# Index scores in units of two heads, their products with the low key parts each on half of TensorE's rows

## The reference, cut to what matters

```python
adm = (kpos[None, :] // CHUNK) <= (qpos[:, None] // CHUNK)
isc = jnp.einsum('bqhd,bsd->bqhs', qib, k_idx) * (IDX_DIM ** -0.5)
score = jnp.einsum('bqhs,bqh->bqs', jax.nn.relu(isc), wb * (IDX_HEADS ** -0.5))
score = jnp.where(adm[None], score, NEG)
_, idx = lax.top_k(score, n_sel)
```

## Time and profile before

| | us |
|---|---|
| median of three runs | 3438.98 (3437.29 to 3440.9) |
| the profiled execution, its own time | 3442.62 |
| its span in the trace | 3440.8 |
| TensorE busy (PE) | 3356.9, 98% |
| VectorE busy (DVE) | 1940.1, 56% |
| ScalarE busy (ACT) | 1450.8, 42% |
| GpSimd busy (POOL) | 1610.3, 47% |

### The profile page before, as it was taken

One profiled execution on the slowest core, in us unless ns is written; L12 is line 12 of the kernel. 1 busy time (PEld: TensorE's weight loads), 2 busy tenths in 40 slices (PEclk: granted clock), 3 DMA queues, 4 the chain that ended last, 5 costly groups with the idle time before them and its releaser, 6 DMA issues.

```text
span 3440.8 us, 44189 instructions
## 1 busy us (share of the span) xinstructions
PE 3356.9 (98%) x16616; PEld 2774.7 (81%) x16616; DVE 1940.1 (56%) x3380; ACT 1450.8 (42%) x2601; POOL 1610.3 (47%) x949
## 2 busy tenths in 40 slices
PE   7999999999999999999999999999999999999998
PEld 6778878878887888888788878977887789878787
DVE  3236647558565566457667755766768478621112
ACT  3224435345444443245455434735654357420001
POOL 4555554454325555522555552044556510356665
PEclk9999999999999999999999999999999999999999
DMA  4745454444433333323433232063233400432332
GB/s 135 208 138 167 113 168 129 130 129 142 165 105 127 100 103 96 115 75 135 140 94 109 93 110 87 1 216 97 92 103 100 148 32 1 136 103 92 93 103 92
DMA packets 446564, 389.04 MB, mean 113 GB/s; under 512 B 20977, under 2 KB 376561, under 8 KB 445713
## 3 DMA queue, kind: packets, MB, share of 16 engines
q1 hardware_dynamic: 424736, 348.04, 33.1%
q10 hardware_dynamic: 21616, 38.17, 3.1%
HBM read 323.37 MB, written 62.78 MB: 112 GB/s over the span
## 4 chain that ended last, share of the span: by engine, by line
PE 90%; DVE 3%; ACT 3%; issue 1%; DMA 1%; POOL 1%; ACTq 0%; SPq 0%; DVEq 0%; POOLq 0%
PE BANK L800 20%; PE BANK L801 20%; PE BANK L802 20%; PE LP L800 3%; PE LP L802 3%; PE LP L801 3%; PE BANK L1013 3%; PE BANK L1028 2%; PE LP L990 2%; PE LP L991 2%; PE BANK L1030 2%; PE LP L892 2%; PE LP L891 2%; PE LP L996 1%; PE BANK L1039 1%
## 5 line engine op out<-in xcount | busy, mean ns | idle before, releaser
L768 POOL TENSOR_SCALAR WHI<-WRAW 128x1024 fp32r<-128x1024 f32 x456 | 494.8, 1085 | 1424.4 <-PE BANK L802 1164.7
L770 POOL TENSOR_TENSOR WLO<-WRAW,WHI 128x1024 fp32r<-128x1024 f32 x456 | 1108.7, 2431 | 38.0
L800 PE MATMUL BANK<-H2hi,WHI 128*128 128x512 f32 x1408 | 565.5, 402 | 3.6 <-DVE X L2036 3.6
L801 PE MATMUL BANK<-H2lo,WHI 128*128 128x512 f32 x1408 | 558.2, 396 | 0.0
L802 PE MATMUL BANK<-H2hi,WLO 128*128 128x512 f32 x1408 | 557.4, 396 | 0.0
L800 PE MATMUL BANK<-HThi,WHI 128*128 128x512 f32 (+1 forms) x1024 | 408.9, 399 | 1.8 <-DVE QS L1634 1.8
L801 PE MATMUL BANK<-HTlo,WHI 128*128 128x512 f32 (+1 forms) x1024 | 404.9, 395 | 0.0
L802 PE MATMUL BANK<-HThi,WLO 128*128 128x512 f32 (+1 forms) x1024 | 404.6, 395 | 0.0
L1384 ACT ACTIVATE MASK<-SCD,THR 128x896 bf16<-128x896 f32 (+5 forms) x186 | 281.9, 1516 | 227.3 <-DVE THR L1693 199.7
L802 PEld LDWEIGHTS BANK<-H2hi,WLO 128*128 128x128 f32 x1408 | 265.3, 188 | 65.0
L800 PEld LDWEIGHTS BANK<-H2hi,WHI 128*128 128x128 f32 x1408 | 265.8, 189 | 62.7 <-DVE X L2036 4.5
(11 more groups left out here) (279 smaller groups left out, 6504.7 us busy)
## 6 DMA issues: line engine op xcount, KB each, us to landing
WRAW<-in_w_in SPq DMA_DIRECT2D x124, 512.0 KB, 4.4
WRAW<-in_w_ffn_gate SPq DMA_DIRECT2D x88, 512.0 KB, 3.8
WRAW<-in_w_ffn_up SPq DMA_DIRECT2D x88, 512.0 KB, 3.8
WRAW<-in_w_ffn_down SPq DMA_DIRECT2D x88, 512.0 KB, 3.8
qsp<-QS SPq DMA_DIRECT2D x32, 512.0 KB, 5.7
gates<-GS ACTq DMA_DIRECT2D x64, 256.0 KB, 2.1
WRAW<-in_w_out SPq DMA_DIRECT2D x32, 512.0 KB, 4.1
GL<-gates ACTq DMA_DIRECT2D x48, 256.0 KB, 4.1
```

The lines of the kernel that those rows point to most:

```text
L768: nc.gpsimd.tensor_scalar(hi, raw, 1.0, 1.0, ALU.mult, ALU.mult).then_inc(w_hi, 1)
L770: nc.gpsimd.tensor_tensor(lo, raw, hi.bitcast(f32), ALU.subtract).then_inc(w_split, 1)
L800: nc.tensor.matmul(dst, whi, mhi, start=first, stop=False)
L801: nc.tensor.matmul(dst, whi, mlo, start=False, stop=False)
```

## The change

A unit is now two heads (2m and 2m + 1) of one query tile over up to 512 keys, each head in a bank of its own of the LP buffer. The two products with KIhi stay as they were, over 128 rows. Of the products with KIlo only the query's high part is kept, 64 rows: for the even head rows 0 to 63, for the odd head rows 64 to 127. The product of low query by low key is left out. In the built program these two matmuls carry the position (0, 0) and (64, 0) and the size 64 by 128. The relu takes both heads in one instruction, the additions are two per unit, each of up to 512 columns.

```diff
         def score_units(b):
-            return [(b, j, h, c, w) for j in searched(b) for h in range(HEADS) for c, w in chunks(width_of(b, j))]
+            return [(b, j, m, c, min(ROWS, width_of(b, j) - c)) for j in searched(b) for m in range(HEADS // 2)
+                    for c in range(0, width_of(b, j), ROWS)]
...
-                for _, j, h, c, w in score_units(b):
-                    dst = take("logits", relu_ready, (b, j, h, c), ("idx", b, j, h, c))
-                    for a, v in halves(c, w):
-                        q = Q[:, h, j * P:(j + 1) * P]
-                        nc.tensor.matmul(dst[:, a - c:a - c + v], q, KIhi[:, a:a + v], start=True, stop=False)
-                        last = nc.tensor.matmul(dst[:, a - c:a - c + v], q, KIlo[:, a:a + v], start=False, stop=True)
-                    last.then_inc(logits_full, made(logits_full, ("idx", b, j, h, c)))
+                for _, j, m, c, w in score_units(b):
+                    dst = take("logits", relu_ready, (b, j, m, c), ("idx", b, j, m, c))
+                    for s in range(2):
+                        nc.tensor.matmul(dst[:, s * ROWS:s * ROWS + w], Q[:, 2 * m + s, j * P:(j + 1) * P], KIhi[:, c:c + w],
+                                         start=True, stop=False)
+                    for s in range(2):
+                        r = slice(s * HD, (s + 1) * HD)
+                        nc.tensor.matmul(dst[:, s * ROWS:s * ROWS + w], Q[r, 2 * m + s, j * P:(j + 1) * P], KIlo[r, c:c + w],
+                                         start=False, stop=True).then_inc(logits_full, 1)
+                    made(logits_full, ("idx", b, j, m, c), 2)
                     yield
...
                     if g >= 2:
-                        act.wait_ge(score_added, g - 1)
+                        act.wait_ge(score_added, 2 * (g - 1))
                     act.wait_ge(logits_full, n(logits_full, ("idx",) + key))
-                    nc.scalar.activation(RB[:, g % 2, 0:w], logits(("idx",) + key)[:, 0:w], ACT.Relu
+                    pair = logits(("idx",) + key)[:, :].rearrange("p (s c) -> p s c", s=2)
+                    nc.scalar.activation(RB[:, g % 2, :].rearrange("p (s c) -> p s c", s=2)[:, :, 0:w], pair[:, :, 0:w], ACT.Relu
                                          ).then_inc(relu_ready, made(relu_ready, key))
...
-                    r, iw = RB[:, g % 2, 0:w], IW[:, j, h:h + 1]
                     s = scores_at(b, j)[:, c:c + w]
...
+                    for h in (2 * m, 2 * m + 1):
+                        r, iw = RB[:, g % 2, h % 2 * ROWS:h % 2 * ROWS + w], IW[:, j, h:h + 1]
+                        if h == 0:
+                            ins = nc.vector.tensor_scalar(s, r, iw, None, ALU.mult)
+                        else:
+                            dve.wait_ge(score_added, n(score_added, (b, j, h - 1, c)))
+                            ins = nc.vector.scalar_tensor_tensor(s, r, iw, s, ALU.mult, ALU.add)
+                        ins.then_inc(score_added, made(score_added, (b, j, h, c)))
```

More of the change, by code:

```diff
@@ L1365, in relus @@
             def relus(b):
-                for _, j, h, c, w in score_units(b):
-                    key = (b, j, h, c)
+                for _, j, m, c, w in score_units(b):
+                    key = (b, j, m, c)
                     g = n(relu_ready, key) - 1
                     if g >= 2:
-                        act.wait_ge(score_added, g - 1)
+                        act.wait_ge(score_added, 2 * (g - 1))
                     act.wait_ge(logits_full, n(logits_full, ("idx",) + key))
-                    nc.scalar.activation(RB[:, g % 2, 0:w], logits(("idx",) + key)[:, 0:w], ACT.Relu
+                    pair = logits(("idx",) + key)[:, :].rearrange("p (s c) -> p s c", s=2)
+                    nc.scalar.activation(RB[:, g % 2, :].rearrange("p (s c) -> p s c", s=2)[:, :, 0:w], pair[:, :, 0:w], ACT.Relu
                                          ).then_inc(relu_ready, made(relu_ready, key))
@@ L1868, in sums @@
             def sums(b):
-                for _, j, h, c, w in score_units(b):
-                    if (h, c) == (0, 0) and j == searched(b)[0]:
+                for _, j, m, c, w in score_units(b):
+                    if (m, c) == (0, 0) and j == searched(b)[0]:
                         dve.wait_ge(iw_ready, n(iw_ready, b))
@@ L1875, in sums @@
                             dve.wait_ge(sc_out, n(sc_out, (b - 1, JT - 1)))
-                    key = (b, j, h, c)
-                    g = n(relu_ready, key) - 1
+                    g = n(relu_ready, (b, j, m, c)) - 1
                     dve.wait_ge(relu_ready, g + 1)
-                    r, iw = RB[:, g % 2, 0:w], IW[:, j, h:h + 1]
                     s = scores_at(b, j)[:, c:c + w]
[L1881 to L1886, removed]
+                    for h in (2 * m, 2 * m + 1):
[6 more added lines that the diff above has]
+                        ins.then_inc(score_added, made(score_added, (b, j, h, c)))
                     top = width_of(b, j)
                     if h == HEADS - 1 and c + w == top:
-                        dve.wait_ge(score_added, n(score_added, key))
+                        dve.wait_ge(score_added, n(score_added, (b, j, h, c)))
                         nc.vector.memset(scores_at(b, j)[0:HD, top - HD:top], NEG).then_inc(score_ready, made(score_ready, (b, j)))
```

## The result

| | before | after |
|---|---|---|
| median, us | 3438.14 (4 runs, 3437.05 to 3440.9) | 3464.73 (4 runs, 3460.47 to 3465.52) |
| the profiled execution, its own time | 3442.62 | 3460.47 |
| its span in the trace | 3440.8 | 3458.6 |
| granted clock, mean over the span | 0.994 | 0.996 |

The ratio is 1.0073, 95% interval 1.0061 to 1.0085: 26.6 us slower, with 21 to 29 us as the interval. I had forecast 3481 with a range of 3452 to 3500. The sign and the range were right, the size was too large by 16 us. The third rival, "the low pair starts together", had 3464.

The account below looks back on a forecast made before the run. TensorE was taken as the bound; four unit sizes added 29.1, 5.0, 4.4 and 3.5 us, 42 in sum, so 3439 + 42 = 3481 us (chance 0.50), with a range of 3452 to 3500.

Parts of the forecast that it names:

- The third rival: Score matmuls: both low matmuls of a unit start together, the second low load costing nothing; +25, 3464 us, chance 0.10.
- TensorE sets the pace: Block 3's score slots: PE busy 159.65 of 160 us, so a unit's PE time changes the span while DVE keeps up.
- What bounds the gain: 31 us: Score matmuls: two 64-row matmuls side by side save one step of four per unit, at most 31 us in all.
- The drain of 0.09 and the open load of 0.11: At each change between 128 and 64 rows: 0.09 us running out, then 0.11 us loading; read at the L940 transposes.
- rival 1: Changes of size in a unit: no drain there, so the kernel gets faster, 3418 to 3428 us; chance 0.16.
- rival 5: Score units: neither drain nor overlap, four steps as before; 3439 us, chance 0.07.
- I stay with 0.11: Low pair: the second low matmul starts 0.11 us after the first, for its load; 152 x 0.11 = 17 us.
- m + 2s + 0.51: Predicted unit time in us: m the step between the high matmuls, s the time one matmul's columns are taken in.
- Rival 2: Low pair: the two low matmuls run one after the other without overlap; +55, 3494 us, chance 0.12.
- VectorE costs nothing: Block 3: five units take DVE 9.94 us against PE's 11.5, so the longer PE stretch covers DVE's extra 14 us.
- rival 4: Block 3: DVE becomes the bound, its doubled additions each meeting a stall, 12.5 us per five units; +52, 3491, chance 0.05.
- 2.4 us of stall: Block 3's last query tile before: four additions in a row take 1.89 us each, not 1.28; the excess was left in.

Follow-up runs that it names:

- experiment 1: The changed kernel with the low products of both heads again over 128 rows, units still in pairs of heads: 3441.67 us, ratio 1.0011.
- Experiment 2: The kernel before, units of one head, with both high matmuls first, then the low ones on that head's 64 rows: 3503.38 us, ratio 1.0190.
- experiment 3: The changed kernel with two units issued together, four high matmuls then two low pairs, per change to 64 rows: 3461.46 us, ratio 1.0071.

## Why the prediction was right in its sign and too large

**TensorE sets the pace.** Right. PE is busy 159.95 of 160 us in block 3, the time followed PE's work to 2 us (27.9 worked out, 26.6 measured), and experiment 1 brought it back with that work.

**What bounds the gain: 31 us.** Right: the pair overlaps fully, a unit of 512 keys has three steps and two changes, 3 x 0.23 + 2 x 0.20 = 1.09.

**The drain of 0.09 and the open load of 0.11, taken from one place with 8 rows and plain float32.** Right, though it was one case of another type and size. Into the low pair it is 650.70 - 650.61 = 0.09; out of it, the L895 truly start at 650.70 + 0.11 and have their columns in at 651.03, and the load starts at 651.13: 0.10. The open load behind it is 651.24 - 651.13 = 0.11. That a price of 8 rows holds for 64 the prediction could only assume; here it does. Experiment 2 gives the same 0.40 for both changes with no overlap in it. The rule of the Trainium skill (TensorEngine Tiling (Array Packing), section Tiling Modes), that a change of tiling mode drains TensorE, is borne out here for 64 rows; the price is that of these rows. With that rival 1, no drain, falls, and rival 5 with it.

**"I stay with 0.11 because that is the distance of two loads right behind such a change".** This is the step that failed. The 0.11 between two loads in the earlier trace rows belongs to two loads on the same rows: experiment 2 has it again (0.29 us for the two, 0.19 for one). After the change they stand on different rows, and the two loads and the two matmuls start together, 4 ns apart. So a unit is m + 2s + 0.40 instead of m + 2s + 0.51: 1.07, 0.905, 0.74 and 0.62 us, where the trace has 1.086, 0.918, 0.749 and 0.627. The term was 152 x 0.11 = 17 us and measured about nothing; 42 - 17 = 25. The 4 ns of the Trainium skill (TensorE: Matmul & The Clock Gate, section Packing small matmuls) are what the trace shows, and the estimate of +26 by that page was the better one. I had the two values side by side and gave 0.50 to the one from this kernel's rows and 0.10 to the other; but the row didn't show the case in question, loads on separate rows.

**Rival 2, one after the other.** Fell; what it would have looked like is experiment 2.

**VectorE costs nothing, rival 4.** Right in what it costs, not in all of its parts. These are additions of the last query tile after, for the earlier trace rows, in the timeline, merged and then one by one with what GpSimd does beside them, and in the groups by shape:

```profile
866.06 10.08 DVE L1890 SCALAR_TENSOR_TENSOR SCP<-RB,IW,SCP 128x512 f32<-128x512 f32 x10 [1.20 <-ACT RB L1377]
877.08 10.08 DVE L1890 SCALAR_TENSOR_TENSOR SCP<-RB,IW,SCP 128x512 f32<-128x512 f32 x10 [0.94 <-ACT RB L1377]
```

```profile
867.05 2.69 POOL L771 TENSOR_TENSOR WLO<-WRAW,WHI 128x1024 fp32r<-128x1024 f32 x1
867.54 2.75 DVE L1890 SCALAR_TENSOR_TENSOR SCP<-RB,IW,SCP 128x512 f32<-128x512 f32 x1
870.22 0.74 DVE L1890 SCALAR_TENSOR_TENSOR SCP<-RB,IW,SCP 128x512 f32<-128x512 f32 x1
```

```profile
L1890 DVE SCALAR_TENSOR_TENSOR SCP<-RB,IW,SCP 128x512 f32<-128x512 f32 x189 | 204.7, 1091 | 56.5 <-ACT RB L1377 52.3
```

Five units take VectorE 10.08 us (predicted 9.94) and TensorE 877.08 - 866.06 = 11.02 us (predicted 11.5), so there is 0.9 us of slack. The mean of an addition is 1.09 us, but few take that long: eight of the ten in the first row take 0.75, as one does alone, and two take 1.45 and 2.75, while GpSimd splits a weight piece. It is so in the whole trace after: of the 196 additions of 512 columns (7 of them in block 0) 144 take 0.75 us and none of them overlaps an L771; the 52 longer ones all do. This is also the "2.4 us of stall" that the prediction left as it was: of its "1.89 each" before, the four take 1.82, 3.43, 1.27 and 1.27 us. It was right to leave it, and rival 4's reason, a stall for each of twice as many instructions, doesn't hold: there is one split a job, however many additions stand beside it. That the one engine holds up the other is argued from this overlap; no run took the splits away.

From block 3's sum of squares to the end of its last addition VectorE is busy for 124.20 us before and 139.96 after, 16 more where I had 14. Over the whole kernel it is 38.5 more, since blocks 0 to 2 have 64 additional instructions as well, which I didn't count. PE didn't wait for it beyond the 0.5 us above. The cover that I named, TensorE's longer slot, is what hides this: with the slot back at 10.2 us, experiment 1 shows 2.4 us of waits, and in experiment 3 VectorE becomes part of the bound.

**The signs named for the trace.** The load of the first L895 starts 0.31 us after the second L891 (some 0.3 predicted); the next matmul of the job truly starts at 651.24, 0.42 after the L895's 650.70 + 0.11 (0.4); PE is busy for 99% in block 2 (233.98 of the 235 us from 483 on); no waits for RB beyond that half microsecond. Two missed: the distance of the two L895, and the second phase "as long as before", which was 7 us shorter in the profiled execution by the granted clock alone.

## What to carry to other kernels

Splitting TensorE's rows for a pair of small matmuls saves one matmul per pair and costs a way in and a way out: 0.23 against 0.40 us here with 512 columns of fp32r, so two pairs per stay only break even. Fewer columns didn't help: a unit lost 0.17 us with 512 columns, 0.24 with 384, 0.28 with 256 and 0.17 with 128. Count the changes of size, not the matmuls, and group before splitting; then ask which buffers that grouping empties at once, since a group that needs all of them waits for the slowest consumer. And where a price is taken over from a row, look whether the row has the very thing that the change alters: here the two loads shared their rows, and the changed ones don't.

## What the runs showed that was not expected

- Two loads on different halves of the rows start together and take 0.19 us as one row of the trace; two on the same half take 0.29.
- The drain has the same length for 8 rows in plain float32 and 64 rows in fp32r, 0.09 to 0.10 us after the columns are in, for 64 rows in both directions.
- Making TensorE's units in block 3 cheaper by 0.2 us each than in the change (experiment 3) made the block longer, 178.8 us against 169.8 and, before, 159.0: PE waited 17.3 us for RB between 90 and 900 us, and 3.4 us went to the lower clock that followed its pauses.
- Additions of VectorE with the same shape take 0.75 us, and up to 2.8 us while GpSimd splits a weight piece (L771, 2.7 us there and 2.4 elsewhere). A mean over them, 1.01 to 1.09 us, describes neither.
